# Where the lead takes its gathered rows: 24 and 10 in place of 14 and 20

## What is computed

```python
def peer_ffn(h, w_q, keys1, keys2, u, v):      # T tokens, 8 heads, top 16 of 128*128 experts
    v1, i1 = lax.top_k(s1, PEER_TOPK)
    v2, i2 = lax.top_k(s2, PEER_TOPK)
    ...
    top, pos = lax.top_k(cand, PEER_TOPK)
    eidx = jnp.take_along_axis(cidx, pos, axis=-1)
    gate = jax.nn.softmax(top, axis=-1)
    ug = u[eidx]
    act = jax.nn.gelu(jnp.einsum('thkd,td->thk', ug, ht)) * gate
    vg = v[eidx]
    return jnp.einsum('thk,thkd->td', act, vg)
```

## Time and profile before

| | us |
|---|---|
| median of 3 runs | 1616.5 |
| lowest, highest | 1612.46, 1620.25 |
| the profiled execution | 1622.78 |
| its span | 1621.0 |
| PE busy, share of the span | 1552.4 (96%) |
| DVE busy | 1386.9 (86%) |
| ACT busy | 607.8 (37%) |
| POOL busy | 509.5 (31%) |

### The profile page before, as it was taken

One profiled execution on the slowest core, in us unless ns is written; L12 is line 12 of the kernel. 1 busy time (PEld: TensorE's weight loads), 2 busy tenths in 40 slices (PEclk: granted clock), 3 DMA queues, 4 the chain that ended last, 5 costly groups with the idle time before them and its releaser, 6 DMA issues.

```text
span 1621.0 us, 23318 instructions
## 1 busy us (share of the span) xinstructions
PE 1552.4 (96%) x8442; PEld 1312.4 (81%) x8442; DVE 1386.9 (86%) x2957; ACT 607.8 (37%) x980; POOL 509.5 (31%) x427
## 2 busy tenths in 40 slices
PE   6999999889999999999899999999999999999997
PEld 6555555468799999998899989989899999777885
DVE  1694796769899967899599999989999999898997
ACT  2111442422255555544233333333333333434433
POOL 1000000044110110022355555555555555344330
PEclk9999899979999999999899999999999999999998
DMA  8482332023055566789999999999999999999993
GB/s 312 143 292 90 132 118 91 26 78 131 22 180 183 177 217 209 230 286 308 376 372 406 391 402 405 405 401 385 404 398 405 402 394 384 364 376 396 397 395 136
DMA packets 175586, 454.66 MB, mean 280 GB/s; under 512 B 14904, under 2 KB 73392, under 8 KB 173424
## 3 DMA queue, kind: packets, MB, share of 16 engines
q1 hardware_dynamic: 108224, 229.74, 39.1%
q0 software_dynamic: 58176, 211.87, 34.0%
q10 hardware_dynamic: 9072, 11.56, 2.1%
HBM read 420.58 MB, written 32.24 MB: 279 GB/s over the span
## 4 chain that ended last, share of the span: by engine, by line
PE 60%; DVE 7%; DMA 3%; ACT 1%; issue 1%; DVEq 0%; ACTq 0%
PE peer_psum L1616 17%; PE peer_psum L1620 8%; PE peer_psum L1676 6%; PE peer_psum L1683 6%; PE peer_psum L1691 6%; PE peer_psum L1663 4%; PE peer_psum L1680 3%; PE peer_psum L1686 3%; PE peer_psum L1628 3%; PE peer_psum L1601 2%; DMA s_all<-in_peer_v 2%; DVE s_all L1798 2%; PE peer_psum L1609 1%; DVE s_all L1794 1%; DVE hT L1758 1%
## 5 line engine op out<-in xcount | busy, mean ns | idle before, releaser
L1616 PE MATMUL peer_psum<-hH,hi_slots 128*128 128x320 f32 x1024 | 309.6, 316 | 7.2 <-DVE lo_slots L1909 2.8
L1616 PE MATMUL peer_psum<-hL,hi_slots 128*128 128x320 f32 x1024 | 304.1, 311 | 0.0
L1487 POOL DMA_INDIRECT hT<-in_peer_u,eidx x128 | 150.9, 1179 | 308.7 <-DVE dots L1758 267.2
L1523 ACT ACTIVATE hi_slots<-s_all 128x1024 fp32r<-128x1024 f32 x128 | 135.9, 1061 | 187.6 <-PE peer_psum L1691 159.2
L1487 POOL DMA_INDIRECT hT<-in_peer_v,eidx x128 | 150.0, 1172 | 178.0 <-DVE s_all L1767 164.5
L1616 PEld LDWEIGHTS peer_psum<-hH,hi_slots 128*128 128x128 f32 x1024 | 194.3, 190 | 12.0 <-issue 6.2
L1616 PEld LDWEIGHTS peer_psum<-hL,hi_slots 128*128 128x128 f32 x1024 | 194.5, 190 | 2.9
L1620 PE MATMUL peer_psum<-hH,lo_slots 128*128 128x320 f32 x1024 | 171.8, 310 | 0.0
L1895 DVE TENSOR_TENSOR lo_slots<-s_all,hi_slots 128x1024 fp32r<-128x1024 f32 x128 | 156.7, 1224 | 17.0 <-ACT hi_slots L1523 16.9
L1767 DVE SCALAR_TENSOR_TENSOR s_all<-hT,coef,s_all 128x1024 f32<-128x1024 f32 x126 | 161.7, 1283 | 3.3 <-DMA hT<-in_peer_v,eidx 2.6
L1620 PEld LDWEIGHTS peer_psum<-hH,lo_slots 128*128 128x128 f32 x1024 | 158.0, 189 | 3.3
(11 more groups left out here) (315 smaller groups left out, 2973.4 us busy)
## 6 DMA issues: line engine op xcount, KB each, us to landing
ring<-in_peer_u SPq DMA_DIRECT2D x128, 512.0 KB, 7.5
s_all<-in_peer_v SPq DMA_DIRECT2D x128, 512.0 KB, 7.0
gate_table<-lot SPq DMA_DIRECT2D x16, 1280.0 KB, 6.7
lot<-gate_table SPq DMA_DIRECT2D x16, 1280.0 KB, 11.2
lot<-in_w_mod SPq DMA_DIRECT2D x5, 2048.0 KB, 8.9
x_sb<-in_w_mod POOLq DMA_DIRECT2D x10, 1024.0 KB, 5.5
gelu_table<-s_all ACTq DMA_DIRECT2D x56, 160.0 KB, 3.7
s_in<-gelu_table SPq DMA_DIRECT2D x56, 160.0 KB, 8.7
```

Source lines behind the costliest of these rows:

```text
L1487: pool.indirect_dma_start(rows_of(j), None, A[table][0], bass.IndirectOffsetOnAxis(eidx[:, k:k + 1], 0)).then_inc(rows_in[j % RG], 16)
L1523: func(H[:, slot_of(w), :], vb[:, w % RING, :], ACT.Copy).then_inc(v_hi, 1)
L1616: mm(ps[:, bank, 0:TD], H[:, b, c * P:(c + 1) * P], h[:, c, T0:T], start=(c == 0 and h is hH), stop=False)
```

## The change

The numbers of rows in the two stretches of the lead are 24 and 10 in place of 14 and 20. Their sum stays 34, so every later turn takes the same rows as before.

```diff
-ROWS_LEAD, ROWS_TAIL = (14, 20), 68
+ROWS_LEAD, ROWS_TAIL = (24, 10), 68
```

## The result

| | before | after |
|---|---|---|
| median of 9 runs each, us | 1616.57 | 1609.43 |
| lowest, highest | 1612.45, 1621.15 | 1601.1, 1612.16 |
| the profiled execution | 1622.78 | 1612.16 |
| its span | 1621.0 | 1610.4 |

The ratio is 0.9944, with a 95% interval of 0.9921 to 0.9966. The changed kernel is faster, by 7.1 us between the medians. The forecast was 1610.3, 0.9 us above the measured median. A ratio of 0.9944 lies just beyond the bound of 0.5% that the prediction set; it had given "within 0.5%" the larger chance.

The account below looks back on a forecast made before the run. It took DVE to bound the second stretch, with PE the bound once rows leave. Gains of 5.6 and 0.6 us, with cost 0 in the first stretch, took 1616.5 to 1610.3 us; range for 8 in 10: 1604 to 1616.

Parts of the forecast that it names:

- Second stretch, 5.6 us: Turns 41 to 50: with eight rows fewer DVE falls just under PE, so ten turns go from 77.53 to 71.9 us.
- The thin margin of 0.04 us for a turn: Turns 41 to 50: a one-row turn takes DVE 7.15 us against PE's 7.19; if not held, gain some 4.5.
- DVE's low halves: Sign of being right: in turns 41 to 50 they stand 7.19 us apart, as PE's transposes do.
- First stretch, cost 0: Ten more rows, 11.4 us of DVE work, fit into DVE's waits around the second tile's settle and in turns 29 to 37.
- the prediction's own sign of being wrong: First stretch: a DMA wait ahead of L1758 before 573 us that moves the settle (L1774) past 574.5.
- row 10 lies ready at 570 to 572: Ahead of the second tile's settle: its gather, issued once row 4 is done at 564.0, lands in 5.9 to 8.1 us.
- rival D: Second tile's settle comes late through row 10's gather and the clock falls: 1618.3, up to 1621 us; chance 0.04.
- The other five rows: Turns 29, 31, 33, 35 and 37: their 5.7 us fit into DVE's 10.0 us of waits ahead of steps; cost 0.
- Lead's end, 0.6 us with bounds of 0 and 1.3: Turns 50 and 51 have two rows fewer, so less DMA traffic delays the gelu store that ACT's last gelu waits for.
- rival C: Lead's end: shorter PE idle time may keep the clock at 2.4 GHz, 3 us more gain, 1606.6 us; chance 0.19.
- B: First stretch, 558 to 575 us: early gathers crowd DMA engines and delay gelu's stores, 1 to 3 us; chance 0.13.
- E: PE's gain is returned at the lead's end, where DMA engines bound the loads: 1616.5 us; chance 0.04.

Follow-up runs that it names:

- e1: Kernel before with 14 and 10 rows in the lead in place of 14 and 20, the ten rows going behind the lead: 1624.35 us, ratio 1.0030.
- e3: Kernel before with DVE multiplying only 512 of 1024 columns of rows 14 to 33, all gathers kept: 1614.62 us, ratio 0.9966.
- e4: Kernel before with the gathers of rows 20 to 39 replaced by loads of 64 columns, DVE's work kept: 1618.31 us, ratio 0.9999.
- e7: Changed kernel driven further, 28 and 6 rows in place of 24 and 10: 1612.99 us, ratio 0.9953 to the kernel before.
- e6: Changed kernel with two rows moved from turns 22 and 24 to turns 50 and 51: 1609.87 us, ratio 0.9936 to the kernel before.
- b1: Kernel before, no edit, traced again: 1616.51 us.
- b2: Kernel before, no edit, traced once more: 1619.84 us.
- a2: Changed kernel, no edit, timed and traced a second time: 1610.89 us, ratio 0.9954 to the kernel before.
- e5: Changed kernel with five rows moved from turns 16 to 24 to turns 27 to 31, behind the settle: 1614.17 us, ratio 0.9966 to the kernel before.
- e1b: The 14 and 10 rows of e1 again, on another chip: 1616.94 us, ratio 0.9987 to the kernel before.
- e8: Changed kernel with 28 and 10 rows, placed by hand around the settle, four fewer behind the lead: 1609.72 us, ratio 0.9957 to the kernel before.

## Why the prediction came out right, step by step

**Second stretch, 5.6 us: right, in size and cause.** Measured 77.53 to 71.92. e1 gives it with this half of the change alone, e3 with half of DVE's work and every gather, and e4, with the traffic gone and the work kept, does not. The thin margin of 0.04 us for a turn held everywhere. One sign was told wrongly: DVE's low halves stand 7.16 apart, its own pace, and not PE's 7.19. That PE is the bound from there on is shown by e7: four rows fewer, and not 0.1 us less.

**First stretch, cost 0: a step failed, and luck kept the price low.** The settle starts at 574.32 and 573.77, not at 572.7 to 573.3; 0.2 us more, and the first would have met the prediction's own sign of being wrong. The step "row 10 lies ready at 570 to 572" failed: it came at 573.17 and 572.62 in two traces, though row 4 was done 1.4 us sooner than I had it. Two durations were off. The prediction let POOL issue a gather as soon as row 4 was done, but POOL came 1.2 us late, since issues took 1.7 to 2.0 us each there; and the landing took 9.3 us where I had read 5.9 to 8.1 (8.0 in the second trace). The room was as predicted, PE wanted the result some 1.8 us after the settle could have come, and so the price was 1.7 us in one execution and 0.04 in the other. This is rival D's mechanism, stopped before its point; D's clock fall did not come with it. It did in e7, at another place. The other five rows cost nothing, as said: DVE's waits ahead of L1794 shrank by 4.5 us.

**Lead's end, 0.6 us with bounds of 0 and 1.3: mechanism half right, size too small.** The term that was mis-sized is this one. In the traces the stage went from 38.5 to 40.2 (three of before) to 34.7 and 36.2 (two of after); the means differ by 4.2. The store no longer holds gelu, which is the full 1.3, and the clock then does not fall for turn 56, which is what rival C had priced at 3 (in the chain the sixteen matmuls fell by 2.0 us and the eight behind them by 0.7). C was given 0.19 and came true in the traces of after, with a fall behind the second idle time in one of them.

The cause named for it, two rows fewer in turns 50 and 51, is not borne out: e6 puts them back, and 0.3 us of the 4.2 returns. e3 keeps all gathers and lets DVE keep up, and the store is on time. e4 keeps DVE late and takes the gathers away, and the store is on time too. So in these traces the store was late only where both came together, a DVE behind PE and the full number of gathers in the second stretch. But e3 and e4 ran on one other chip and e6 on a third, and no trace of the kernel before was taken on either, so that this is not shown beyond these traces. The only traces of before and after known to be from one chip are b1, b2 and a2. How the two make one store late was not taken further apart.

**The sum.** The traces give 5.6 + 4.2 - 0.9 (the mean of 1.7 and 0.04), 8.9 us, and the medians 7.1 in the first series and 6.4 in the second (1617.25 to 1610.89). The forecast of 6.2 is nearer to the timed runs than the sum of what the traces show, and there it was helped by luck: the second term was 3.6 us too small, the first stretch's 0.9 was left out, and a part of the lead's gain doesn't show in the timed runs. Only the 5.6 was right for its reasons. e4 points the same way: 5 us at the lead's end in its trace, none in its time. How much of the lead's end the timed runs gain is open.

**The other rivals.** B, gathers that crowd gelu's stores near 570: no gelu waits for a store in the first stretch in the trace of after. What crowding there was hit the gathers themselves. E, a gain returned at the lead's end: the opposite happened in the traces.

**What stays open.** The price of ten rows behind the lead: in timed runs on the same chip 10.2 us (e1 against e5, 1624.35 - 1614.17) and 7.1 (e1b against e6, 1616.94 - 1609.87), in the traces' fifth column 3.6 to 5.1 over the mean of after and a2, which e7 reaches without those rows. DVE is favoured over traffic and not shown. And whether any placement beats the changed kernel: e6 (0.9936), e8 (0.9957), e7 (0.9953) and the two series of after (0.9944, 0.9954) overlap.

## What to carry to other kernels

When one engine is full in a stage, price the relief by the next engine's own pace: here DVE gave up 9.1 us and PE could take 5.6, and going further gave nothing. When work with prefetched inputs is moved into a gap, the work has to fit and so do its transfers: with six buffers, a run of more than six rows is limited by issue plus landing, and both get longer in the very run that is being made. A difference at a place that the change hardly touches (here a store and the clock) needs a second trace of both kernels before it is put into a sum.

## What the hardware showed that was not expected

An indirect DMA takes POOL 0.94 us to issue alone and 1.68 to 1.99 us in the run, while DVE does one row after the other. Issues that fell into DVE's wait, as those from 570.10 to 572.58, took 0.94 again. It is not enough that DVE is busy: the issue at 557.12 lies beside a reduction of DVE with one input (L1866, 556.76 to 558.57) and took 0.94, the one at 552.26 beside two instructions with two inputs in SBUF (L1862 and L1864) and took 2.28. The Trainium skill says in GPSIMD Engine Reference, section Specifications, that GpSimd's SBUF interfaces are shared with VectorE and that an instruction of DVE with two SBUF inputs contends with it. A row is such an instruction, and the trace agrees with that as far as the times go; no run here changed the number of inputs and nothing else.

PE's clock at the lead's end held through an idle time of 1.5 us in all eleven traces that have it (after and every experiment but b1 and b2), and fell behind one of 2.50 to 2.85 in all three traces of before. Behind the second idle time, 2.1 to 2.2 us, it fell in four of the eleven (after, e1, e3, e5) and held in seven, among them a2, the same kernel as after. That is the whole of the 1.5 us between about 34.7 and 36.2 in the column of the lead's end. Three of the four are from one chip, on which e4 held; the six traces from two other chips all held. Whether the chip has a part in it was not tested. The length of one idle time does not decide it either: in e7 the clock fell to 0.54 behind waits of 1.63 and 0.47 us close together. The Trainium skill's TensorE: Matmul & The Clock Gate, section What's actually happening, has half rate as the default that activity releases. The traces agree in so far as the clock fell behind idle times of PE at these places; from which idle time on it falls they do not settle.
